# Modulation columns of a two-block transformer kernel: block transposes and row sums on VectorE, with one final TensorE sum for all 48 columns

## The chip, the cores and the metric

The kernel runs on one core of a Trainium2 chip. The metric is the device time of one execution in microseconds (us); lower is better. All data are float32 in memory. A core has a matrix engine (TensorE, "PE" in the profile, its weight loads "PEld"), a vector engine (VectorE, "DVE"), a scalar engine (ScalarE, "ACT"), a general engine (GpSimd, "POOL"), and a queue that issues most DMA transfers (SyncE, "SP"). Each engine works through its own list of instructions in order and waits at semaphores for the others.

## The reference, cut to what matters

Two transformer blocks follow one another on 512 tokens of width 1024. The second block begins by making six modulation vectors of width 1024 from a conditioning vector `c`:

```python
cond = jax.nn.silu(c)
for l in range(DEPTH):          # DEPTH = 1
    mod = cond @ ada_w[l] + ada_b[l]          # (1, 1024) @ (1024, 6144)
    shift_m, scale_m, gate_m, shift_f, scale_f, gate_f = jnp.split(mod[:, None, :], N_MOD, axis=-1)

    h = rms_norm_2(x, mix_norm_g[l]) * (1 + scale_m) + shift_m
    proj = h @ w_in[l] + b_in[l]
```

`ada_w` has 6144 columns: 48 groups of 128. `mod` depends on nothing of the first block, so the kernel computes it beside the first block's feed-forward part, and needs it when the second block's first normalisation starts.

## The kernel before

The activations are kept transposed, with channels on the 128 partitions and the 512 tokens along the free axis. The large products run in `tile` (lines 2135 to 2137): for each 128-row slice k, three matmuls with 512 columns, high weights with high activations, high weights with low activations, low weights with high activations. SP loads weights for two tiles at a time into `raw` (function `unit`), ScalarE makes the high part (`hi`, lines 855 and 1125) as soon as the tile four places back is done (`tile_done`), and GpSimd makes the low part (`lo`, line 788, counted by `lo_done`). There are two `raw` buffers and four pairs `w_hi`, `w_lo`.

The tiles that matter here are, in order: the output projection (tiles S_OUT, `into_split_norm(0)`), a normalisation done in halves, the up-projection of the first block (`ffn_pe`, two tiles per VectorE step in a loop of ten rounds with four tiles each), and the down-projection, 24 tiles numbered n = 0 to 23 (`down_part`, the last four in halves by `down_half`). Tile n = 18 has eight slices. Every sixth and fifth down tile is followed by `residual2` on VectorE (line 1822), ScalarE's `square2` (line 1155), and VectorE's `add_square2` (lines 1833, 1834). ScalarE does `square2` for n = 5, 6, 11, 12, 17 and 18 ahead of the `hi` of tile n + 4, in its fixed order.

The modulation works on column group n, from 0 to 47:

- SP loads 128 columns of `ada_w_2`, 1024 rows deep, into `ada[n % 2]`, 512 KB (`ada_load`, line 698). From n = 2 on it first waits until `ada_summed` has reached n - 1, that is until group n - 2 is reduced and its buffer free. These loads stand between the weight loads in SP's one list, so one that waits holds the next weight load back.
- VectorE (`ada_reduce`) multiplies the eight slices by their `cond` column and adds them: one TENSOR_SCALAR (line 1746), six SCALAR_TENSOR_TENSOR into PSUM bank 5 (line 1751), and one that writes the sum to SBUF as `ada_sum` (line 1756), after which `ada_summed` rises.
- TensorE (`ada_tile`, line 2440) sums over the partitions: `ada_sum` as weights against a column of ones. The result is one column of PSUM bank 6. The profile records it as two passes.

Groups 0 to 5 stand in the output projection and the normalisation, 6 to 27 in the up-projection (two per round), and 28 to 47 among the down tiles: VectorE reduces them at its steps n = 0 to 15, TensorE turns them into columns after tiles n = 0 to 17. Then VectorE waits for all 48 (`ada_done`), adds `ada_b_2` (line 1850) and makes the gains. Group 27 is the last one of the loop; `count` in the code is only the semaphore's value.

Of the kernel before, what the change touches and what calls it, by code (L numbers as in the profile page):

```python
# [10 lines left out]
ALU = mybir.AluOpType  # L11
ACT = mybir.ActivationFunctionType
AX = mybir.AxisListType


P = 128
# [142 lines left out]
def build(nc, a, out):  # L159
# [5 lines left out]
    with ctx:  # L165
# [100 lines left out]
        g_lo = sb("g_lo", [P, FT, T], F32R)  # L266
        ada_at = offset[0]
        ada = [sb(f"ada{n}", [P, KD, P], at=ada_at + 4096 * n) for n in range(2)]
        ada_sum = [sb(f"ada_sum{n}", [P, P], at=ada_at + 8192 + 512 * n) for n in range(2)]
        ua = sq  # L270
        uv = hn
        assert max(top1, ada_at + 9216) <= end
# [1077 lines left out]
        def _(dve):  # L1350
# [383 lines left out]
            def ada_reduce(n, loaded, i=None):  # L1734

                buf = n % 2
                count = lambda v: v if i is None else i * 2 + v

                acc = ps[5][:, 0:P]
                if n:  # L1740
                    dve.wait_ge(ada_summed, count(n))
                dve.wait_ge(ada_in[buf], loaded)
                for k in range(KD):
                    src, c = ada[buf][:, k, :], cond[:, k:k + 1]
                    if k == 0:
                        dve.tensor_scalar(acc, src, c, None, ALU.mult).then_inc(ada_scaled, 1)
                        continue
                    done = (KD - 1) * n + k
                    dve.wait_ge(ada_scaled, done if i is None else i * (2 * (KD - 1)) + done)
                    if k < KD - 1:  # L1750
                        dve.scalar_tensor_tensor(out=acc, in0=src, scalar=c, in1=acc, op0=ALU.mult,  # L1751
                                                 op1=ALU.add).then_inc(ada_scaled, 1)
                        continue
                    if n >= 2:
                        dve.wait_ge(ada_done, count(n - 1))
                    dve.scalar_tensor_tensor(out=ada_sum[buf][:, :], in0=src, scalar=c, in1=acc, op0=ALU.mult,
                                             op1=ALU.add).then_inc(ada_summed, 1)

            def ada_between_halves():
                dve.wait_ge(half_lo, KD)  # L1760
# [77 lines left out]
            for n in range(20):  # L1838
                if n % 6 >= 4:
                    dve.wait_ge(tile_done, S_DOWN + n + 1)  # L1840
                    residual2(n, slice(0, T)).then_inc(freed["dve"], 1)
                if n < 16:
                    for _ in range(2 if n % 4 == 2 else 1):
                        m = next(next_ada)
                        ada_reduce(m, 16 * (m // 2 + 1))
                if n >= 6 and n % 6 in (0, 1):
                    add_square2((n - 6) // 6 * 2 + n % 6)

            dve.wait_ge(ada_done, NMOD * KD)
# [282 lines left out]
        def _(pe):  # L2132
# [62 lines left out]
            def into_split_norm(b, x, xl, ready, after=lambda n: None):  # L2195

                s0 = SPLIT_FROM[b]
                if b == 2:

                    for part in ((0, 4), (4, KD)):  # L2200
                        for n in range(2):
                            tile(s0 + n, x, xl, part=part, ready=ready if n == 0 else None)
                for n in range(2 if b == 2 else 0, 4):
                    tile(s0 + n, x, xl, ready=ready if n == 0 else None)
                    after(n)
                for n in range(4, KD):
                    half_tile(b, s0 + n, 0, x, xl)
                    after(n)
# [11 lines left out]
            def parts(sem, base=0):  # L2220
                return lambda k: pe.wait_ge(sem, base + k + 1)
# [212 lines left out]
            for s in range(S_CONV, S_OUT):  # L2434
                tile(s, cv_hi, cv_lo, ready=parts(cv_lo_done) if s == S_CONV else None)

            def ada_tile(n, buf, count):

                pe.wait_ge(ada_summed, count)
                pe.matmul(ps[6][:, bass.ds(n, 1)] if not isinstance(n, int) else ps[6][:, n:n + 1],  # L2440
                          ada_sum[buf][:, :], ones[:, 0:1], start=True, stop=True).then_inc(ada_done, 1)

            def early_ada(tile_n):
                n = {1: 0, 2: 1, 3: 2, 5: 3, 6: 4}.get(tile_n)
                if n is not None:
                    ada_tile(n, n % 2, n + 1)

            into_split_norm(0, h_hi, h_lo, parts(freed["dve"], FREED[S_CONV][1] - 1), early_ada)

            def ffn_pe(s0, b):  # L2450
                for half in range(2):
                    for j in range(4):
                        if (half, j) == (1, 0):
                            second_halves(s0, h_hi, h_lo, lambda k: pe.wait_ge(half_lo, PIECES * b + KD + k + 1))
                        if half and j < 2:
                            continue
                        half_tile(b, s0 + j, half, h_hi, h_lo,
                                  ready=(lambda k: pe.wait_ge(half_lo, PIECES * b + KD * half + k + 1)) if j == 0 else None)
                        if (half, j) == (0, 1):
                            second_sum(b)  # L2460
                        if (half, j) == (1, 3) and b == 0:
                            ada_tile(ADA_EARLY - 1, (ADA_EARLY - 1) % 2, ADA_EARLY)
                with pe.Fori(0, FT // 2 - 1) as i:
                    for j in range(4):
                        s = s0 + 4 + j
                        pe.wait_ge(lo_done, i * 4 + (s + 1))
                        pe.wait_ge(freed["dve"], i * 4 + (FREED[s][1] - 4))
                        for k in range(KD):
                            ins = split_product(ps[BANK[s]][:, :], w_hi[s % 4][:, k, :], w_lo[s % 4][:, k, :],
                                                h_hi[:, k, :], h_lo[:, k, :], k == 0, k == KD - 1)  # L2470
                        ins.then_inc(tile_done, 1)
                        if b == 0 and j % 2:
                            n = ADA_EARLY + j // 2
                            ada_tile(i * 2 + n, n % 2, i * 2 + (n + 1))

            ffn_pe(S_UP, 0)

# [44 lines left out]
            next_ada = itertools.count(ADA_EARLY + ADA_UP - 2)  # L2522
            for n in range(20):
                down_part(S_DOWN, n, parts(g_lo_done, 2) if n in (0, 2, 4) else None)
                if n < 18:
                    for _ in range(2 if n and n % 4 == 0 else 1):
                        m = next(next_ada)
                        ada_tile(m, m % 2, m + 1)
            for n in range(20, 24):
                down_half(n, 0)  # L2530
            for n in range(20, 24):
# [248 lines left out]
```

## Time and profile before

| quantity | value |
|---|---|
| median of 3 runs | 1382.02 us (1380.93 to 1382.14) |
| profiled execution, its own time | 1381.31 us |
| span of the profiled execution | 1379.3 us |
| PE busy | 1367.5 us |
| DVE busy | 770.4 us |
| ACT busy | 599.2 us |
| POOL busy | 600.4 us |
| transfers over the span | 106 GB/s |

Busy time is a union over the span, so the engines overlap. Matmuls are pipelined, and their recorded durations overlap too; how long TensorE takes for a row of them is read from start to start.

### The profile page before, as it was taken

To read this page: it belongs to the slowest core of one execution; us is meant where nothing else is said; L and a number is where in the kernel's file an instruction comes from. 1 tells how busy PE (TensorE), PEld (TensorE's weight loads), DVE (VectorE), ACT (ScalarE), POOL (GpSimd) and SP (SyncE) were. 2 spreads that over 40 slices of the span, in tenths; PEclk is the share of its full clock that TensorE was granted. 3 is DMA by queue.
4 is the path that set the end of the run, shared out by engine and by line. 5 is a ranking of instruction groups with operands and counts; after the bars stand their busy time and mean duration, and the time that the engine had idled before them with its cause. 6 is when DMAs were issued, how large, how long until landed. Compare 5 with 4: busy or idle time off the path is not lost.

```text
span 1379.3 us, 20888 instructions
## 1 busy us (share of the span) xinstructions
PE 1367.5 (99%) x7650; PEld 1142.9 (83%) x7650; DVE 770.4 (56%) x1524; ACT 599.2 (43%) x1030; POOL 600.4 (44%) x322
## 2 busy tenths in 40 slices
PE   8999999999999999999999999999999999999998
PEld 7877777778998888888889978878998888888887
DVE  5897965456677566666873868633563223231222
ACT  6223555464254445443222524575364434442222
POOL 7532222226254444444543479623354444444441
PEclk9999999999999999999999999999999999999999
DMA  6931011015525444445662141021223332222221
GB/s 214 228 93 62 31 62 46 25 38 168 168 94 166 139 147 150 146 129 170 196 203 92 62 122 62 32 62 31 92 78 106 106 107 91 91 87 96 99 84 62
DMA packets 188309, 146.15 MB, mean 106 GB/s; under 512 B 21561, under 2 KB 186659, under 8 KB 188240
## 3 DMA queue, kind: packets, MB, share of 16 engines
q1 hardware_dynamic: 186528, 144.59, 34.0%
q8 instruction: 47, 0.77, 0.2%
q10 hardware_dynamic: 1200, 0.36, 0.1%
q0 software_dynamic: 512, 0.25, 0.1%
q14 instruction: 22, 0.18, 0.0%
HBM read 143.08 MB, written 2.10 MB: 105 GB/s over the span
## 4 chain that ended last, share of the span: by engine, by line
PE 91%; DVE 5%; DMA 3%; issue 1%; ACT 0%; DVEq 0%; ACTq 0%
PE ps L2135 27%; PE ps L2137 26%; PE ps L2136 26%; DMA ada<-in_ada_w 3%; DVE ps L1751 2%; PE ps L2584 2%; PE ps L2324 2%; PE ps L2379 1%; PE ps L2408 1%; PE ps L2655 1%; PE ps L2611 1%; PE ps L2640 1%; PE ps L2677 0%; PE ps L2218 0%; PE ps L2570 0%
## 5 line engine op out<-in xcount | busy, mean ns | idle before, releaser
L788 POOL TENSOR_TENSOR w_lo<-raw,w_hi 128x1024 fp32r<-128x1024 f32 (+2 forms) x224 | 515.4, 2304 | 709.0 <-ACT w_hi L855 439.4
L2135 PE MATMUL ps<-h_hi,w_hi 128*128 128x512 f32 (+1 forms) x1336 | 504.0, 377 | 0.6 <-DVE h_lo L1386 0.6
L2136 PE MATMUL ps<-h_lo,w_hi 128*128 128x512 f32 (+1 forms) x1336 | 493.4, 369 | 0.0
L2137 PE MATMUL ps<-h_hi,w_lo 128*128 128x512 f32 (+1 forms) x1336 | 493.2, 369 | 0.0
L2135 PEld LDWEIGHTS ps<-h_hi,w_hi 128*128 128x128 f32 x1336 | 251.7, 188 | 60.8 <-issue 17.6
L2137 PEld LDWEIGHTS ps<-h_hi,w_lo 128*128 128x128 f32 x1336 | 251.8, 188 | 43.1
L2136 PEld LDWEIGHTS ps<-h_lo,w_hi 128*128 128x128 f32 x1336 | 251.9, 189 | 40.1 <-issue 0.5
L855 ACT ACTIVATE w_hi<-raw 128x1024 fp32r<-128x1024 f32 (+2 forms) x136 | 133.7, 985 | 254.5 <-PE ps L2137 245.1
L1125 ACT ACTIVATE w_hi<-raw 128x1024 fp32r<-128x1024 f32 x88 | 93.2, 1059 | 217.9 <-PE ps L2137 217.9
L2135 PE MATMUL ps<-g_hi,w_hi 128*128 128x512 f32 (+1 forms) x394 | 146.6, 372 | 0.0
L2136 PE MATMUL ps<-g_lo,w_hi 128*128 128x512 f32 (+1 forms) x394 | 144.6, 367 | 0.0
L2137 PE MATMUL ps<-g_hi,w_lo 128*128 128x512 f32 (+1 forms) x394 | 144.4, 367 | 0.0
L1751 DVE SCALAR_TENSOR_TENSOR ps<-ada,cond,ps 128x128 f32<-128x128 f32 x288 | 102.5, 356 | 10.3
L2137 PEld LDWEIGHTS ps<-g_hi,w_lo 128*128 128x128 f32 x394 | 74.3, 188 | 12.2
L2135 PEld LDWEIGHTS ps<-g_hi,w_hi 128*128 128x128 f32 x394 | 74.3, 189 | 11.7
L2136 PEld LDWEIGHTS ps<-g_lo,w_hi 128*128 128x128 f32 x394 | 74.4, 189 | 11.5
L1790 DVE SCALAR_TENSOR_TENSOR sq<-ps,small,sq 128x511 f32<-128x511 f32 x44 | 33.0, 750 | 88.4 <-ACT sq L1132 85.4
L2060 DVE SCALAR_TENSOR_TENSOR xT<-ps,small,xT 128x256 f32<-128x256 f32 (+1 forms) x22 | 13.3, 604 | 106.1 <-PE ps L2137 106.1
L1527 DVE SCALAR_TENSOR_TENSOR ps<-z,small,ps 128x512 f32<-128x512 f32 x106 | 70.4, 747 | 0.0
L1784 DVE TENSOR_TENSOR hn<-ps,sq 128x512 f32<-128x512 f32 x22 | 15.2, 691 | 85.9 <-ACT sq L1136 85.9
L1022 ACT ACTIVATE sc<-sc,stat 128x128 f32<-128x128 f32 (+3 forms) x64 | 35.5, 555 | 35.0 <-DVE stat L1540 34.9
L1670 DVE COPY pT<-ps 128x128 f32<-128x128 f32 (+3 forms) x32 | 15.7, 490 | 54.3 <-PE ps L2379 32.1
(362 smaller groups left out, 1700.8 us busy)
## 6 DMA issues: line engine op xcount, KB each, us to landing
ada<-in_ada_w SPq DMA_DIRECT2D x48, 512.0 KB, 3.8
raw<-in_ffn_w_up SPq DMA_DIRECT2D x22, 1024.0 KB, 4.9
raw<-in_w_up SPq DMA_DIRECT2D x22, 1024.0 KB, 4.9
raw<-in_w_in SPq DMA_DIRECT2D x21, 1024.0 KB, 5.0
raw<-in_ffn_w_down SPq DMA_DIRECT2D x8, 896.0 KB, 6.2
raw<-in_w_down SPq DMA_DIRECT2D x8, 896.0 KB, 4.7
raw<-in_w_in SPq DMA_DIRECT2D x16, 256.0 KB, 3.8
raw<-in_w_out SPq DMA_DIRECT2D x4, 1024.0 KB, 5.2
```

Of the source, the lines that this page charges most:

```text
L788: pool.tensor_tensor(w_lo[slot % 4][:, 0:nk, :], part[:, :, slot % 2 * P:(slot % 2 + 1) * P], w_hi[slot % 4][:, 0:nk, :].bitcast(F32), ALU ...
L855: act.activation(w_hi[s % 4][:, 0:nk, :], part[:, :, s % 2 * P:(s % 2 + 1) * P], ACT.Copy).then_inc(hi_done, 1)
L1022: act.activation(x, x, ACT.Exp, scale=-1.0, bias=stat[:, 2 * (j % 2) + g:2 * (j % 2) + g + 1], accum_out=stat[:, 4 + 2 * (j % 2) + g:5 + 2 ...
L1125: act.activation(w_hi[s % 4][:, :, :], part[:, :, s % 2 * P:(s % 2 + 1) * P], ACT.Copy).then_inc(hi_done, 1)
L1527: ins = dve.scalar_tensor_tensor(out=out, in0=src, scalar=w, in1=was, op0=ALU.mult, op1=ALU.add)
L1751: dve.scalar_tensor_tensor(out=acc, in0=src, scalar=c, in1=acc, op0=ALU.mult, op1=ALU.add).then_inc(ada_scaled, 1)
L1790: dve.scalar_tensor_tensor(out=u[:, t, 1:T], in0=src[:, 0:T - 1], scalar=col(wname, m + wide), in1=u[:, t, 1:T], op0=ALU.mult, op1=ALU.add ...
L2135: pe.matmul(out_ap, w, x, start=first, stop=False, **kw)
L2136: pe.matmul(out_ap, w, xl, start=False, stop=False, **kw)
L2137: return pe.matmul(out_ap, wl, x, start=False, stop=last, **kw)
L2324: pe.matmul(ps[4 + g][:, 0:L], qT[grp, i, t * P:(t + 1) * P], kT[grp, b, 0:L], start=True, stop=True).then_inc(qk_done, 1)
L2584: ins = pe.matmul(bank[:, at:at + nq], keys[:, hd, t * P:(t + 1) * P], qd[n % 2][:, hd, q0:q0 + nq], start=True, stop=True)
```

## The change

`ada_reduce` keeps the whole sum in PSUM: the eighth slice is added there as well. VectorE then transposes the 128x128 sum in 32x32 blocks, into the second quarter of bank 5, and adds up the 32 elements of each row of a block, which leaves four numbers per partition. They go to PSUM bank 6, at column 256 + 4n, and `ada_summed` rises after that. The partition group j of 32 and the four columns together hold partial sums of the 128 outputs. After group 47, `ada_columns` copies the 192 numbers per partition to SBUF (`ada_parts`) and makes `stacked`, a 128x32 matrix of four identities of size 32, from `ident`. TensorE no longer runs `ada_tile`; after tile n = 18 `ada_sums` runs four matmuls with `stacked` as weights and 48 columns each, one for each 32 output partitions. SP's code is the same. The core of the diff:

```diff
-        ada_sum = [sb(f"ada_sum{n}", [P, P], at=ada_at + 8192 + 512 * n) for n in range(2)]
+        ada_parts = sb("ada_parts", [P, 4, NMOD * KD], at=ada_at + 8192)
+        stacked = sb("stacked", [P, 32], at=ada_at + 8192 + 4 * 4 * NMOD * KD)
...
-                acc = ps[5][:, 0:P]
+                acc, turned = ps[5][:, 0:P], ps[5][:, P:2 * P]
+                step = lambda k: (KD + 1) * n + k
+                wait_step = lambda k: dve.wait_ge(ada_scaled, step(k) if i is None else i * (2 * (KD + 1)) + step(k))
                 if n:
-                    dve.wait_ge(ada_summed, count(n))
+                    wait_step(0)
                 dve.wait_ge(ada_in[buf], loaded)
                 for k in range(KD):
...
-                    if k < KD - 1:
-                        dve.scalar_tensor_tensor(out=acc, in0=src, scalar=c, in1=acc, op0=ALU.mult,
-                                                 op1=ALU.add).then_inc(ada_scaled, 1)
-                        continue
-                    if n >= 2:
-                        dve.wait_ge(ada_done, count(n - 1))
-                    dve.scalar_tensor_tensor(out=ada_sum[buf][:, :], in0=src, scalar=c, in1=acc, op0=ALU.mult,
-                                             op1=ALU.add).then_inc(ada_summed, 1)
+                    wait_step(k)
+                    dve.scalar_tensor_tensor(out=acc, in0=src, scalar=c, in1=acc, op0=ALU.mult,
+                                             op1=ALU.add).then_inc(ada_scaled, 1)
+                wait_step(KD)
+                if n:
+                    dve.wait_ge(ada_summed, count(n))
+                dve.transpose(turned, acc).then_inc(ada_scaled, 1)
+                wait_step(KD + 1)
+                first = 2 * P + 4 * n
+                dve.tensor_reduce(ps[6][:, first:first + 4] if i is None else ps[6][:, bass.ds(i * 8 + first, 4)],
+                                  turned.rearrange("p (j c) -> p j c", c=32), AX.X, ALU.add).then_inc(ada_summed, 1)
+
+            def ada_columns():
+
+                dve.wait_ge(ada_summed, NMOD * KD)
+                dve.tensor_copy(ada_parts[:, :, :], ps[6][:, 2 * P:2 * P + 4 * NMOD * KD].rearrange("p (n j) -> p j n", j=4))
+                dve.tensor_reduce(stacked[:, :], ident[:, :].rearrange("p (i r) -> p r i", r=32), AX.X,
+                                  ALU.add).then_inc(ada_summed, 1)
...
+                if n == 16:
+                    ada_columns()
...
-            dve.wait_ge(ada_done, NMOD * KD)
+            dve.wait_ge(ada_done, 1)
...
-            def ada_tile(n, buf, count):
-
-                pe.wait_ge(ada_summed, count)
-                pe.matmul(ps[6][:, bass.ds(n, 1)] if not isinstance(n, int) else ps[6][:, n:n + 1],
-                          ada_sum[buf][:, :], ones[:, 0:1], start=True, stop=True).then_inc(ada_done, 1)
+            def ada_sums():
+
+                pe.wait_ge(ada_summed, NMOD * KD + 1)
+                for j in range(4):
+                    ins = pe.matmul(ps[6][32 * j:32 * (j + 1), 0:NMOD * KD], stacked[:, :], ada_parts[:, j, :],
+                                    start=True, stop=True)
+                ins.then_inc(ada_done, 1)
...
             for n in range(20):
                 down_part(S_DOWN, n, parts(g_lo_done, 2) if n in (0, 2, 4) else None)
-                if n < 18:
-                    for _ in range(2 if n and n % 4 == 0 else 1):
-                        m = next(next_ada)
-                        ada_tile(m, m % 2, m + 1)
+                if n == 18:
+                    ada_sums()
```

VectorE at the end of the down-projection, before: the last two groups (46 and 47), the residuals of tiles 16 and 17, and the squares.

```order
550 L1746 TENSOR_SCALAR ps<-ada_111,cond 128x128
551 L1751 SCALAR_TENSOR_TENSOR ps<-ada_111,cond,ps 128x128 x6
552 L1756 SCALAR_TENSOR_TENSOR ada_sum_113<-ada_111,cond,ps 128x128
553 L1746 TENSOR_SCALAR ps<-ada_112,cond 128x128
554 L1751 SCALAR_TENSOR_TENSOR ps<-ada_112,cond,ps 128x128 x6
555 L1756 SCALAR_TENSOR_TENSOR ada_sum_114<-ada_112,cond,ps 128x128
556 L1822 TENSOR_TENSOR xT<-ps,xT 128x512 x2
557 L1833 TENSOR_TENSOR rstd<-hn,rstd 128x512
```

The same place in the changed kernel, whose line numbers are a little higher.

```order
584 L1749 TENSOR_SCALAR ps<-ada_111,cond 128x128
585 L1752 SCALAR_TENSOR_TENSOR ps<-ada_111,cond,ps 128x128 x7
586 L1757 STREAM_TRANSPOSE ps<-ps 128x128
587 L1760 TENSOR_REDUCE ps<-ps 128x4
588 L1749 TENSOR_SCALAR ps<-ada_112,cond 128x128
589 L1752 SCALAR_TENSOR_TENSOR ps<-ada_112,cond,ps 128x128 x7
590 L1757 STREAM_TRANSPOSE ps<-ps 128x128
591 L1760 TENSOR_REDUCE ps<-ps 128x4
592 L1833 TENSOR_TENSOR xT<-ps,xT 128x512
593 L1766 COPY ada_parts<-ps 128x192
594 L1767 TENSOR_REDUCE stacked<-ident 128x32
595 L1833 TENSOR_TENSOR xT<-ps,xT 128x512
```

Each group has two VectorE instructions more, and the copy and the reduction of `ada_columns` stand between the residuals of tiles 16 and 17.

TensorE after down tile n = 16, before: the columns of groups 45 and 46 stand between the last matmul of tile 16 and the first of tile 17.

```order
2239 L2137 MATMUL ps<-g_hi,w_lo_57 128x512
2240 L2440 MATMUL ps<-ones,ada_sum_114 128x1
2241 L2440 MATMUL ps<-ones,ada_sum_113 128x1
2242 L2135 MATMUL ps<-g_hi,w_hi_54 128x512
2243 L2136 MATMUL ps<-g_lo,w_hi_54 128x512
```

TensorE in the changed kernel, between tile n = 18 and tile n = 19, the only place where it does something for the modulation.

```order
2252 L2149 MATMUL ps<-g_lo,w_hi_51 128x512
2253 L2150 MATMUL ps<-g_hi,w_lo_55 128x512
2254 L2452 MATMUL ps<-ada_parts,stacked 32x48 x4
2255 L2148 MATMUL ps<-g_hi,w_hi_52 128x512
2256 L2149 MATMUL ps<-g_lo,w_hi_52 128x512
```

The 48 small products that were spread over the first block's second half are gone, and four others wait in one place for all 48 groups.

## Rows read from the trace of the kernel before

**Rows 1.** The page: busy us (share of the span) x instructions of each engine.

```profile
PE 1367.5 (99%) x7650; PEld 1142.9 (83%) x7650; DVE 770.4 (56%) x1524; ACT 599.2 (43%) x1030; POOL 600.4 (44%) x322
```

**Rows 2.** Timeline of PE around one column: start us, duration us, instruction, count.

```profile
432.56 0.39 PE L2137 MATMUL ps<-h_hi,w_lo 128*128 128x512 f32 x1
432.79 0.28 PE L2440 MATMUL ps<-ones,ada_sum 128*128 128x1 f32 x2
432.93 0.48 PE L2135 MATMUL ps<-h_hi,w_hi 128*128 128x512 f32 x1
...
433.48 0.39 PE L2137 MATMUL ps<-h_hi,w_lo 128*128 128x512 f32 x1
...
439.61 0.39 PE L2137 MATMUL ps<-h_hi,w_lo 128*128 128x512 f32 x1
```

**Rows 3.** Waits of PE and PEld, 340 to 740: us in total, times, longest.

```profile
PEld ps L2440 <- DVE ada_sum L1756: 1.3, 2, 1.0
```

**Rows 4.** The chain that ended last, 700 to 737: start us, us, what.

```profile
724.14 0.36 DVE ada_sum L1756
724.54 0.38 PE ps L2440 x2
```

**Rows 5.** Timeline of DVE in the down-projection; in brackets idle us and releaser.

```profile
642.72 0.35 DVE L1746 TENSOR_SCALAR ps<-ada,cond 128x128 f32<-128x128 f32 x1
643.10 2.32 DVE L1751 SCALAR_TENSOR_TENSOR ps<-ada,cond,ps 128x128 f32<-128x128 f32 x6
645.46 0.35 DVE L1756 SCALAR_TENSOR_TENSOR ada_sum<-ada,cond,ps 128x128 f32<-128x128 f32 x1
...
649.04 0.35 DVE L1756 SCALAR_TENSOR_TENSOR ada_sum<-ada,cond,ps 128x128 f32<-128x128 f32 x1
649.48 0.35 DVE L1746 TENSOR_SCALAR ps<-ada,cond 128x128 f32<-128x128 f32 x1
...
654.93 0.35 DVE L1746 TENSOR_SCALAR ps<-ada,cond 128x128 f32<-128x128 f32 x1 [2.36 <-DMA ada<-in_ada_w]
...
675.40 0.35 DVE L1746 TENSOR_SCALAR ps<-ada,cond 128x128 f32<-128x128 f32 x1 [2.98 <-DMA ada<-in_ada_w]
...
699.35 0.35 DVE L1746 TENSOR_SCALAR ps<-ada,cond 128x128 f32<-128x128 f32 x1 [3.29 <-DMA ada<-in_ada_w]
...
708.37 0.35 DVE L1746 TENSOR_SCALAR ps<-ada,cond 128x128 f32<-128x128 f32 x1 [2.34 <-DMA ada<-in_ada_w]
...
727.98 0.35 DVE L1756 SCALAR_TENSOR_TENSOR ada_sum<-ada,cond,ps 128x128 f32<-128x128 f32 x1
728.24 0.69 DVE L1822 TENSOR_TENSOR xT<-ps,xT 128x512 f32<-128x512 f32 x1
```

**Rows 6.** Waits of DVE, 636 to 735: us in total, times, longest.

```profile
DVE ps L1746 <- DMA ada<-in_ada_w: 13.0, 8, 3.3
```

**Rows 7.** Waits of DVE in the up-projection's loop, 405 to 636.

```profile
DVE hn L1790 <- ACT hn L1132: 47.3, 20, 3.8
```

**Rows 8.** Groups of DVE by line: busy us, mean ns, idle us before.

```profile
L1602 DVE TENSOR_REDUCE stat<-cp 128x8 f32<-128x248 f32 x4 | 1.6, 411 | 0.1
L1569 DVE COPY hn<-ps 127x128 f32<-127x128 f32 x2 | 0.5, 278 | 0.0
```

**Rows 9.** Timeline of PE: the first matmul of down tile 19.

```profile
735.38 0.39 PE L2135 MATMUL ps<-g_hi,w_hi 128*128 128x512 f32 x1
```

**Rows 10.** The chain that ended last, 3 to 12: start us, us, what.

```profile
3.56 4.99 PE ps L2218 x22
...
9.83 0.45 PE ps L2218 x4
```

**Rows 11.** Windows: us, busy by engine (x), PEclk, DMA share, GB/s.

```profile
4.00:5.00 1.00, 1.00 (x7) 1.00 (x6) 0.00 (x0) 0.50 (x1) 1.00 (x3) 1.00 1.01 406
```

**Rows 12.** Timeline of ACT where a square waits for VectorE's residual.

```profile
703.07 0.63 ACT L1155 ACTIVATE hn<-xT 128x512 f32<-128x512 f32 x1 [5.46 <-DVE xT L1822]
```

**Rows 13.** Timeline of POOL: the low weights made after that square.

```profile
704.70 2.11 POOL L788 TENSOR_TENSOR w_lo<-raw,w_hi 128x896 fp32r<-128x896 f32 x1 [3.88 <-ACT w_hi L855]
```

More of the change, by code:

```diff
@@ L1747, in ada_reduce @@
                         continue
-                    done = (KD - 1) * n + k
-                    dve.wait_ge(ada_scaled, done if i is None else i * (2 * (KD - 1)) + done)
-                    if k < KD - 1:
-                        dve.scalar_tensor_tensor(out=acc, in0=src, scalar=c, in1=acc, op0=ALU.mult,
-                                                 op1=ALU.add).then_inc(ada_scaled, 1)
-                        continue
-                    if n >= 2:
-                        dve.wait_ge(ada_done, count(n - 1))
-                    dve.scalar_tensor_tensor(out=ada_sum[buf][:, :], in0=src, scalar=c, in1=acc, op0=ALU.mult,
-                                             op1=ALU.add).then_inc(ada_summed, 1)
+                    wait_step(k)
[14 more added lines that the diff above has]
+                                  ALU.add).then_inc(ada_summed, 1)
             def ada_between_halves():
@@ L2193, in second_sum, with into_split_norm @@
                 pe.matmul(ps[7][:, COLS[1]], ones[:, :], rstd[:, COLS[1]], start=True, stop=True).then_inc(summed, 1)
-            def into_split_norm(b, x, xl, ready, after=lambda n: None):
+            def into_split_norm(b, x, xl, ready):
                 s0 = SPLIT_FROM[b]
@@ L2204, in into_split_norm @@
                     tile(s0 + n, x, xl, ready=ready if n == 0 else None)
-                    after(n)
                 for n in range(4, KD):
                     half_tile(b, s0 + n, 0, x, xl)
-                    after(n)
                 for n in range(4, KD):
@@ L2435, in _ @@
                 tile(s, cv_hi, cv_lo, ready=parts(cv_lo_done) if s == S_CONV else None)
-            def ada_tile(n, buf, count):
-                pe.wait_ge(ada_summed, count)
-                pe.matmul(ps[6][:, bass.ds(n, 1)] if not isinstance(n, int) else ps[6][:, n:n + 1],
-                          ada_sum[buf][:, :], ones[:, 0:1], start=True, stop=True).then_inc(ada_done, 1)
[L2443 to L2448, printed above, removed]
+            def ada_sums():
[4 more added lines that the diff above has]
+                ins.then_inc(ada_done, 1)
+            into_split_norm(0, h_hi, h_lo, parts(freed["dve"], FREED[S_CONV][1] - 1))
             def ffn_pe(s0, b):
@@ L2460, in ffn_pe @@
                             second_sum(b)
-                        if (half, j) == (1, 3) and b == 0:
-                            ada_tile(ADA_EARLY - 1, (ADA_EARLY - 1) % 2, ADA_EARLY)
                 with pe.Fori(0, FT // 2 - 1) as i:
@@ L2471, in ffn_pe @@
                         ins.then_inc(tile_done, 1)
-                        if b == 0 and j % 2:
-                            n = ADA_EARLY + j // 2
-                            ada_tile(i * 2 + n, n % 2, i * 2 + (n + 1))
             ffn_pe(S_UP, 0)
@@ L2520, in turn_inverse @@
                 ins.then_inc(inverses_turned, 1)
-            next_ada = itertools.count(ADA_EARLY + ADA_UP - 2)
             for n in range(20):
                 down_part(S_DOWN, n, parts(g_lo_done, 2) if n in (0, 2, 4) else None)
-                if n < 18:
-                    for _ in range(2 if n and n % 4 == 0 else 1):
-                        m = next(next_ada)
-                        ada_tile(m, m % 2, m + 1)
+                if n == 18:
+                    ada_sums()
             for n in range(20, 24):
```

## The prediction

> **What bounds the kernel now.** I read the page first: TensorE is busy for 1367.5 of 1379.3 us, VectorE for 770.4 [rows 1], so work taken from TensorE comes off the time unless someone else takes over as the last. Next the timeline of TensorE around one modulation column, for what a column costs there: the reader is to look at the starts, since durations overlap [rows 2]. Then the waits, for where TensorE already stood still for the modulation: two weight loads waited for VectorE's sum, 1.3 us in all, and nothing larger waits there between 340 and 740 [rows 3]. Small as that is, the chain that ended last shows what it means: it runs through VectorE's last operation of a group at 724.14 into TensorE's column at 724.54 [rows 4]. So in the down-projection VectorE's row of reductions and TensorE end nearly together: VectorE had no lead there. The last view is VectorE's own timeline and waits in that stretch [rows 5, 6]. Some of its reductions wait for their load: 13.0 us in eight waits [rows 6], of which four long ones are 2.36, 2.98, 3.29 and 2.34 [rows 5], 10.97 us together, so that the other four are 2.0 us together.
>
> **What TensorE is relieved of.** Ordinary matmuls follow one another at (439.61 - 433.48) / 27 = 0.227 us. From the matmul before a column (432.56) to the third one after it (433.48) are 0.92 us instead of 3 x 0.227 = 0.68 [rows 2]. A column costs 0.24 us, and 48 cost 11.5 us. The two waits add 1.3 [rows 3]. Left alone, TensorE would start down tile 19 at 735.38 [rows 9] - 12.8 = 722.6.
>
> **What VectorE takes on.** Before, a group runs from the start of its first operation at 642.72 to the end of the last, 645.46 + 0.35 = 645.81: 3.09 us. Inside, a dependent operation of this size starts (645.46 - 643.10) / 6 = 0.39 us after the one before it, with 0.35 of its own: 0.04 us between an end and the next start [rows 5]. The eighth operation stays, now into PSUM. The transposition and the row sum are new, and the trace of before shows neither at this size. The nearest rows are a copy of 128 columns out of PSUM, 0.278 us, and a TENSOR_REDUCE of 248 columns, 0.411 us [rows 8]. The row sum of 128 columns lies between 0.411 x 128/248 = 0.21 and 0.411; I take 0.28, as the copy of 128 columns, whose data are of this size. For the transposition I take 0.30 between the copy's 0.278 and the 0.35 of an operation with a column of scalars [rows 5, 8]; that it runs at half the copy's rate, so up to about twice 0.278, is not excluded. With two gaps of 0.04 the sum is 0.30 + 0.28 + 0.08 = 0.66; since ends in PSUM may come later I take **0.70 us a group**, bounds 0.5 (two times 0.21 and the gaps) and 1.05 (0.56 + 0.41 + 0.08).
>
> The Trainium skill (VectorE: DVE Perf Modes, "The three transpose paths") gives 311 ns for a 128x128 bf16 transposition in blocks, by which a group would cost 0.67. Its "Rules for kernel authors" advise TensorE for 128x128 and warn that `tensor_reduce` is the slowest operation of the engine; no run here has shown that yet.
>
> **Where that is hidden, and where not.** In the up-projection's loop VectorE waits 47.3 us in 20 waits, 3.8 at most, for ScalarE and so for TensorE's tiles [rows 7]; that is over 2 us a wait against 0.70 that comes in front of it. The cost of groups 0 to 27 is covered there and in the normalisation; without this cover each would cost 0.70. TensorE's gain is real until then: VectorE enters the down-projection with the tile that TensorE finished at 633, 25 columns earlier, so 25 x 0.24 = 6.0 us earlier.
>
> In the down-projection 21 groups (27 to 47) follow almost without pause. Only SP's loads loosen the row. SP issues the load of group k when group k - 2 is reduced, so a reduction that was gated by its load inherits the delay of k - 2 and not of k - 1. That gives back one 0.70 at each of the four long waits, 2.8, and at the four short ones only the wait itself, 2.0. Where one group directly follows another, the new group's first operation need no longer wait for the end of the sum (0.44 us from 649.04 to 649.48 [rows 5]), only for the transposition; against the 0.26 between 727.98 and 728.24 [rows 5] that saves 0.18 a time, at four places 0.7. The delay that VectorE gathers is
>
> 21 x 0.70 - 2.8 - 2.0 - 0.7 = 9.2 us,
>
> and 9.2 - 6.0 = 3.2 us later than before its last group is done: 727.98 + 0.35 + 3.2 = 731.5. Behind it come the residual of tile 16 (0.69 [rows 5], of which 0.6 before the next can start), the copy of 192 columns and the reduction for `stacked`, 0.3 each by the same rows: **732.7**. Only then may TensorE run `ada_sums`. It came to that place at 722.6, so it stands still for about 10 us: the gain of 12.8 is turned into a wait. What is queued behind it is tile 19, the last four tiles in halves and everything after.
>
> ScalarE's squares also wait for VectorE's residuals, ahead of the next `hi` in its list. Before, such a square started at 703.07 after 5.46 us of waiting [rows 12], and the low weights behind it were ready at 704.70 + 2.11 = 706.8 [rows 13], 3.7 later. With VectorE's delay of about 7 at that point, less 6, the square comes near 704 to 705 and the weights near 708 to 709; they are for tile 16, which TensorE, free of its columns, reaches at 707 to 708. That is a microsecond or two of waiting before the large wait, which becomes as much shorter: it costs nothing more. SP's weight loads wait behind modulation loads that come later by the same delay; the buffers hold weights for two pairs of tiles ahead, and VectorE's delay against TensorE is smaller than a pair of tiles takes (48 x 0.227 = 10.9 us), so I count nothing. VectorE's reading of `mod` has slack until the halves of tile 22.
>
> **After the wait.** The four products cost 4 x 0.24 = 1.0 us by the columns of before. Tile 19 would start at 733.8 instead of 735.38: 1.6 us gained. But TensorE after 10 us of rest is unlike TensorE at work: at the start of the program, after 3.3 us without work, 22 matmul passes took 4.99 us, 0.227 each, and four of the same kind later took 0.45 us, 0.112 each [rows 10]. The granted clock in the window row reads 1.00 there [rows 11], so here the spacing shows the lower rate and the clock column does not. Half rate for 5 us costs 2.5 us. Nothing in the second half of this trace shows a rest of 10 us, so the bounds are 0 and 2.5; I take the 2.5, by the nearest row. The sum is -1.6 + 2.5 = **+0.9 us** against the profiled execution's own 1381.31 us (span 1379.3), and against the median, which is 0.7 above that execution, 1382.9.
>
> The Trainium skill (TensorE: Matmul & The Clock Gate, "HAM oscillation — how this bites in real kernels") says that idle gaps of the matrix engine put its clock back to the lower of its two levels, 1.2 instead of 2.4 GHz; by that rule the 2.5 us is due, and without it the kernel gains 1.6. The start of this trace agrees in the spacing.
>
> **Rivals.**
> - *The cost of a group is higher.* Each 0.1 us above 0.70 a group adds 21 x 0.1, less 0.4 at the four long waits and some 0.3 at the short ones, which then give back more: 1.4 us. At 0.85 the sum is +3.0, at 1.05 it is +5.8: 1385 to 1388. For it: neither operation is in the trace. Against it: the copy and the reduction that are there are cheap. It decides from 0.84 us a group.
> - *The clock does not fall*, or only shortly: -1.6, or 1380.4; with a group at 0.55 also -3.7, or 1378.3. For it: the granted clock reads 1.00 everywhere. Against it: rows 10.
> - *Faster: the sums stay off the path.* If VectorE's delay were covered, because loads come sooner once SP is relieved or because a group costs hardly more than before, TensorE would keep its 12.8 less 1.0 for `ada_sums`: -11.8, or 1370.2. It needs VectorE to be ready at 722.6, with its last group 6 us before where it now stands and before the copy, while all 8 waits for loads are only 13.0 us. Against it stands that VectorE was already the later one [rows 3, 4].
> - *The wait breaks something behind it*: weights for tiles 20 to 23 late through ScalarE's squares, some 2 to 4 us more. For it: the squares of tiles 16 and 17 stand in ScalarE's list before the weights of tiles 21 and 22. Against it: tile 21 follows the wait by more than tile 19's 24 x 0.227 = 5.4 us, and those weights need 3.7.
>
> **How the numbers follow.** 0.2% of this time is 2.8 us, about what a measurement can tell from no change. The forecast case (a group at 0.6 to 0.83, lower rate after the wait) runs from -0.5 to +2.8: chance 0.42, nearly all "same". Dearer groups 0.28 and the broken wait 0.05: slower. No fall of the clock 0.15, half of it within 0.2%. Off the path 0.10. Same 0.47, slower 0.33, faster 0.20. The range goes from groups at 0.5 with the clock kept (-1.6 - 2.8, or 1377.6) to groups at 1.05 with TensorE's half rate (1388); the forecast case alone is 1381.5 to 1384.8.
>
> **What the profile after would show.** TensorE's instructions 96 passes fewer and 8 more, and its loop round 0.48 us shorter: right if VectorE's entry into the down-projection is 6 us earlier. The transposition near 0.30 and the row sum near 0.28. VectorE's waits for loads down from 13.0 us to some 8 or 9. One long wait of PE for VectorE's `stacked`, 8 to 11 us, ending near 733, and behind it matmuls at twice the 0.227 for up to 5 us. The prediction is wrong if the wait is under 5 us or over 15, if a group costs under 0.5 or over 1.05, or if the matmuls behind the wait run at 0.227 from the first.

## The result

The changed kernel took 1373.97 us (median of 6 runs, 1372.26 to 1376.49) against 1380.73 us for the kernel before in the same series; the ratio is 0.9945, 95% interval 0.9935 to 0.9956. A second series gave 1375.10 against 1381.81, ratio 0.9943 (0.9931 to 0.9956). The change makes the kernel 0.55% faster, some 7 us. The forecast was 1382.9, no change that can be told.

The page of the profiled execution (its own time 1372.39 us), which answers to [rows 1]:

```profile
span 1370.7 us, 20826 instructions
PE 1357.2 (99%) x7562; PEld 1132.7 (83%) x7562; DVE 802.8 (59%) x1622; ACT 598.4 (44%) x1030; POOL 601.6 (44%) x322
```

TensorE has 88 passes fewer (96 less 8), and 10.3 us less of busy time. VectorE has 98 instructions and 32.4 us more.

VectorE's timeline in the down-projection, as in [rows 5]: groups 29 and 30, then two places where the kernel before waited for a load, then the end of group 47 and what follows it.

```profile
640.81 0.35 DVE L1749 TENSOR_SCALAR ps<-ada,cond 128x128 f32<-128x128 f32 x1
641.20 2.71 DVE L1752 SCALAR_TENSOR_TENSOR ps<-ada,cond,ps 128x128 f32<-128x128 f32 x7
643.94 0.33 DVE L1757 STREAM_TRANSPOSE ps<-ps 128x128 f32<-128x128 f32 x1
644.30 0.30 DVE L1760 TENSOR_REDUCE ps<-ps 128x4 f32<-128x128 f32 x1
644.51 0.35 DVE L1749 TENSOR_SCALAR ps<-ada,cond 128x128 f32<-128x128 f32 x1
...
693.28 0.35 DVE L1749 TENSOR_SCALAR ps<-ada,cond 128x128 f32<-128x128 f32 x1
...
701.27 0.35 DVE L1749 TENSOR_SCALAR ps<-ada,cond 128x128 f32<-128x128 f32 x1
...
723.25 0.30 DVE L1760 TENSOR_REDUCE ps<-ps 128x4 f32<-128x128 f32 x1
723.46 0.68 DVE L1833 TENSOR_TENSOR xT<-ps,xT 128x512 f32<-128x512 f32 x1
724.06 0.35 DVE L1766 COPY ada_parts<-ps 128x192 f32<-128x192 f32 x1
724.32 0.37 DVE L1767 TENSOR_REDUCE stacked<-ident 128x32 f32<-128x128 f32 x1
```

A group now lasts from 640.81 to 644.60, 3.79 us instead of 3.09: the 0.70 of the forecast, with 0.33 for the transposition and 0.30 for the row sum. But group 47 ends at 723.55, where the forecast had 731.5. The two rows at 693.28 and 701.27 are groups 41 and 43: there the kernel before waited 3.29 and 2.34 us for the load [rows 5], and here no bracket stands behind them.

VectorE's waits for loads between 636 and 735, in the form of [rows 6] (us in total, times, longest):

```profile
DVE ps L1749 <- DMA ada<-in_ada_w: 3.2, 4, 1.5
```

TensorE's wait for VectorE's last sum, from its waits between 636 and 745, in the form of [rows 3]:

```profile
PE ps L2452 <- DVE stacked L1767: 3.0, 1, 3.0
```

TensorE's timeline at the final products, between tiles 18 and 19:

```profile
721.34 0.39 PE L2150 MATMUL ps<-g_hi,w_lo 128*128 128x512 f32 x1
724.75 0.29 PE L2452 MATMUL ps<-ada_parts,stacked 128*32 128x48 f32 x8 [3.02 <-DVE stacked L1767]
724.97 0.50 PE L2148 MATMUL ps<-g_hi,w_hi 128*128 128x512 f32 x1
725.31 0.40 PE L2149 MATMUL ps<-g_lo,w_hi 128*128 128x512 f32 x1
```

Tile 19 starts at 724.97 instead of 735.38 [rows 9], 10.4 us earlier. Of these 0.7 were there before the change could act: this execution started its first products that much sooner. So the change had won 9.7 us here. The eight passes cost 0.22 us from start to start and not 1.0; they have 32 columns of weights each where the passes of before had 128, but no run here tries that width by itself.

1.6 us went again later. The chain that ended last, near 943:

```profile
942.67 0.43 PE ps L2149
943.10 0.43 PE ps L2150
```

And the window row from 942 to 945, in the form of [rows 11] (in the last column but two the granted clock, the share of TensorE's full rate that it was given):

```profile
942.00:945.00 3.00, 3.00 (x8) 2.35 (x8) 0.28 (x1) 1.91 (x4) 0.00 (x0) 0.50 0.00 0
```

The matmuls follow at 0.43 us instead of 0.23, and the granted clock is 0.50 of full speed, the 1.2 GHz level; before came 24 recorded passes with one column each.

### The profile page after: what moved, and what is told of

Its sections match the earlier page's. It is cut to its first block, busy times and chain, and to the rows that moved or that the text cites. A ratio compares the mean times of both kernels' runs of the same rounds, so it can differ in the third digit from the quotient of the medians.

```text
span 1370.7 us, 20826 instructions
## 1 busy us (share of the span) xinstructions
PE 1357.2 (99%) x7562; PEld 1132.7 (83%) x7562; DVE 802.8 (59%) x1622; ACT 598.4 (44%) x1030; POOL 601.6 (44%) x322
## 4 chain that ended last, share of the span: by engine, by line
PE 90%; DVE 7%; DMA 2%; issue 1%; ACT 0%; DVEq 0%; SPq 0%; ACTq 0%
PE ps L2148 26%; PE ps L2149 26%; PE ps L2150 26%; DVE ps L1752 3%; PE ps L2584 2%; PE ps L2335 2%; PE ps L2390 1%; DMA ada<-in_ada_w 1%; PE ps L2419 1%; PE ps L2655 1%; PE ps L2611 1%; PE ps L2640 1%; DMA x_in<-in_x 0%; PE ps L2677 0%; DVE ps L1757 0%
## 5 line engine op out<-in xcount | busy, mean ns | idle before, releaser
L1752 DVE SCALAR_TENSOR_TENSOR ps<-ada,cond,ps 128x128 f32<-128x128 f32 x336 | 119.6, 356 | 12.0
L2073 DVE SCALAR_TENSOR_TENSOR xT<-ps,small,xT 128x256 f32<-128x256 f32 (+1 forms) x22 | 13.3, 604 | 106.2 <-PE ps L2150 106.2
```

## The experiments

In each, the "row" is VectorE's stretch from the start of group 27 to the end of group 47, read from its timeline, and "load waits" are the waits inside it. "Residuals and squares" are VectorE's eleven operations with 512 columns between these groups: four residuals and seven steps of squares. Theory A: VectorE's extra work is swallowed by the load waits, because loads also land sooner. Theory B is the rule on record, that a load wait gives back one group's extra cost at most. Theory C is chance from one execution to the next.

| kernel | row us | load waits us | residuals and squares us | median flight us | PE waits for a sum us | ratio to before (95%) |
|---|---|---|---|---|---|---|
| before | 88.8 | 13.0 | 11.9 | 4.5 | 1.3 | 1 |
| before_again | 88.5 | 13.5 | 11.2 | 4.3 | 1.0 |  |
| changed | 90.8 | 3.2 | 9.5 | 3.9 | 3.0 | 0.9945 (0.9935 to 0.9956) |
| after_again | 90.6 | 2.3 | 10.0 | 4.1 | 2.9 | 0.9943 (0.9931 to 0.9956) |
| pe_only | 80.7 | 8.8 | 8.1 | 4.1 | 0 | 0.9913 (0.9896 to 0.9929) |
| dve_only | 90.1 | 3.6 | 8.6 | 3.9 | 2.5 | 1.0036 (1.0023 to 1.0048) |
| swapped | 84.3 | 4.7 | 8.7 | 3.8 | 0 | 0.9988 (0.9978 to 0.9997) |
| slow | 98.5 | 0.5 | 13.1 | 4.1 | 10.8 | 0.9988 (0.9978 to 0.9999) |
| sums19 | 90.8 | 1.9 | 11.1 | 4.0 | 0 | 0.9903 (0.9886 to 0.9919) |
| sums19_again | 95.1 | 3.7 | 13.3 | 4.1 | 1.9 | 0.9913 (0.9897 to 0.9929) |
| early_release | 85.7 | 0.8 | 7.5 | 3.9 | 0 | 0.9921 (0.9895 to 0.9947) |
| both | 85.7 | 0.6 | 7.5 | 4.0 | 0 | 0.9908 (0.9891 to 0.9924) |

The flight is a modulation load's time from issue to landing, the median of those issued between 640 and 722. In the kernels that keep TensorE's columns, its waits are those of its weight loads. The five columns before the ratio are of one profiled execution each.

The steps of squares are not of one length, and the traces show with what they change: with GpSimd's making of low weights (`w_lo`). From the kernel before, a residual, with one of its two inputs in PSUM, and a step of a square, with both in SBUF, each beside such an operation; and the same step in the changed kernel:

```profile
660.83 2.12 POOL L788 TENSOR_TENSOR w_lo<-raw,w_hi 128x896 fp32r<-128x896 f32 x1 [1.14 <-ACT w_hi L855]
661.05 0.68 DVE L1822 TENSOR_TENSOR xT<-ps,xT 128x512 f32<-128x512 f32 x1
682.58 2.39 POOL L788 TENSOR_TENSOR w_lo<-raw,w_hi 128x1024 fp32r<-128x1024 f32 x1 [1.89 <-ACT w_hi L855]
682.80 2.73 DVE L1833 TENSOR_TENSOR rstd<-hn,rstd 128x512 f32<-128x512 f32 x1
...
678.08 2.40 POOL L789 TENSOR_TENSOR w_lo<-raw,w_hi 128x1024 fp32r<-128x1024 f32 x1 [2.29 <-ACT w_hi L856]
679.68 1.35 DVE L1844 TENSOR_TENSOR rstd<-hn,rstd 128x512 f32<-128x512 f32 x1
```

Over the 12 profiles, between 636 and 735, 49 steps of squares start while a `w_lo` operation runs: each ends 0.28 to 0.55 us after that operation, and they last up to 2.9 us. The other 80 last 0.48 to 0.75 us. The residuals last 0.68 to 0.69 us, also the twelve that start while a `w_lo` operation runs. So the squares' part of the row depends on how long they meet GpSimd's low weights.

**before_again: the kernel before once more.**

> The unchanged kernel once more. If the load waits of the row are a matter of chance from one execution to the next, they differ from 13.0 us by several us here, and the duration of the row from 88.8 us. If they belong to the program, both stay within 1 us, and so do the landing times of the single loads (6.9 us for group 41, 5.8 for group 43).

The group of modulation loads in the DMA issues from 640 to 722 in the first profile of the kernel before, with the median flight last:

```profile
ada<-in_ada_w SPq DMA_DIRECT2D x19, 512.0 KB, 4.5
```

The same group in before_again:

```profile
ada<-in_ada_w SPq DMA_DIRECT2D x19, 512.0 KB, 4.3
```

And in the changed kernel:

```profile
ada<-in_ada_w SPq DMA_DIRECT2D x18, 512.0 KB, 3.9
```

Row and load waits come out within 0.5 us of the first profile, and so do the flights of groups 41 and 43 (6.4 and 5.9 us instead of 6.9 and 5.8). They belong to the program, and theory C falls for the kernel before, as far as two profiles can tell. What did differ was the clock: this execution dropped to half rate at 952.7 for eleven matmuls and lost 3.2 us against the first one, where the first one did not.

**dve_only: only VectorE's part of the change.** From the kernel before, with TensorE's columns kept; the edit cut to its core, arguments and semaphore steps left out:

```diff
-                    dve.scalar_tensor_tensor(out=ada_sum[buf][:, :], ...).then_inc(ada_summed, 1)
+                    dve.scalar_tensor_tensor(out=ada_sum[buf][:, :], ...).then_inc(ada_scaled, 1)
+                dve.transpose(turned, ada_sum[buf][:, :]).then_inc(ada_scaled, 1)
+                dve.tensor_reduce(ps[5][:, first:first + 4], ...).then_inc(ada_summed, 1)
```

> The kernel before, TensorE's 48 columns kept, but VectorE transposes and row-sums each group as in the change (the four numbers go unused to another bank). By the rule on record (a load wait gives back only one group's extra cost) the row of 21 reductions grows by about 9 us, and TensorE, which waits for each group, is held: 8 to 9 us slower. By the rival (the extra work is swallowed by the 13.0 us of load waits, because loads land sooner when they are spaced wider) the row grows by about 2 us, load waits fall from 13.0 to about 3, and the kernel is 1 to 3 us slower.

VectorE's waits for loads between 636 and 735 in this kernel (us in total, times, longest):

```profile
DVE ps L1748 <- DMA ada<-in_ada_w: 3.6, 5, 1.6
```

VectorE's load waits fell to the 3.6 us of this line, and 21 x 0.70 = 14.7 us more work lengthened the row by 1.3 us. Theory B had 9. The load waits gave back 9.4 us of it; the residuals and squares, shorter by 3.3 us, gave back most of the rest, which theory A did not have. In the profiled execution TensorE reached tile 19 by 1.2 us later than before, counted from its first products; the median over executions is 4.7 us later (1385.31 against 1380.61), which is what neither theory gave (1 to 3, and 8 to 9). The profile shows a drop of the clock near 953 for 1.6 us of the rest. For the remaining 2 us of the median there is no profile; the mean granted clock of these executions was 0.996 to 0.998, that of the kernel before 0.998 to 1.000, so part of it may be lower clock elsewhere.

**pe_only: only TensorE's part.** 47 of the 48 columns are left out, so the second block gets wrong modulation; VectorE works as before, without its waits for the columns. The part of the edit in the down-projection; the columns of groups 0 to 27 are taken out in the same way:

```diff
-                if n < 18:
-                    for _ in range(2 if n and n % 4 == 0 else 1):
-                        m = next(next_ada)
-                        ada_tile(m, m % 2, m + 1)
+                if n == 18:
+                    ada_tile(NMOD * KD - 1, (NMOD * KD - 1) % 2, NMOD * KD)
```

> The kernel before, with VectorE's work as it was, but TensorE makes no modulation column except the last one, after down tile 18 (47 of 48 columns are left out, so the second block is computed with wrong modulation). Both theories agree here: TensorE loses 47 x 0.24 = 11.3 us and its 1.3 us of waits; VectorE's row of 21 reductions in the down-projection, from the start of group 27 to the end of group 47, stays at its 88.8 us within 1.5 us and begins 6 us earlier, so TensorE does not wait at the last column. About 12.5 us faster than before, less what the lower clock takes elsewhere (0 to 3 us).

1368.74 us against 1380.61, 11.9 us faster; in the profile TensorE stood 12.95 us earlier from tile 19 to the end, by the sum 47 x 0.24 + 1.3 = 12.6. The price of the columns was right. The row was not: its work is that of before, and it shrank from 88.8 to 80.7 us. Load waits fell by 4.2 us, and the residuals and squares took 8.1 instead of 11.9 us. What differs for the row is when TensorE's tiles, and with them SP's weight loads and GpSimd's low parts, come beside it.

**swapped: order and spacing of the loads alone.** The kernel before, SP's order in the down-projection changed:

```diff
-                if m % 2:
-                    unit((S_DOWN + 7 + m) // 2)
                 for _ in range(2 if m % 4 == 2 else 1):
                     k = next(next_ada)
                     if k < NMOD * KD:
                         ada_load(k)
+                if m % 2:
+                    unit((S_DOWN + 7 + m) // 2)
```

> The kernel before with one change in SP's list for the down-projection: the weight load of every second step stands behind that step's modulation load instead of ahead of it. VectorE's and TensorE's work is the same. If the loads of before land late because the next modulation load leaves 1 to 3 us behind a weight load (which is my theory of what wider spacing cured in the changed kernel), the mean flight of the loads of the row falls from 4.7 us to about 4.2, load waits from 13.0 to 8 or less, the row from 88.8 us by 3 us or more, and TensorE's 1.3 us of waits vanish: 1 us faster, not more. If spacing is not the cause, flights and waits stay within 1 us.

The waits of VectorE between 636 and 735 in this kernel that bear on the row:

```profile
DVE xT L1822 <- PE ps L2137: 7.0, 3, 4.1
DVE ps L1746 <- DMA ada<-in_ada_w: 4.7, 7, 0.8
DVE ada_sum L1756 <- PE ps L2440: 4.2, 4, 1.5
```

No operation of any compute engine was added or taken away, and the load waits fell from 13.0 to 4.7 us, the row to 84.3, although 7.1 us of it are now waits for TensorE (4.2 for its columns, 2.8 for its tiles), which the row did not have before; the squares took 3.2 us less. TensorE's 1.3 us of waits are gone; the kernel gained 0.12%, as expected. So the load waits depend on when the loads leave. SP's timeline shows it, in the kernel before around group 41, whose load had a flight of 6.9 us:

```profile
689.21 0.37 SPq L698 DMA_DIRECT2D ada<-in_ada_w  x1
690.20 0.37 SPq L688 DMA_DIRECT2D raw<-in_ffn_w_down  x1
692.40 0.37 SPq L698 DMA_DIRECT2D ada<-in_ada_w  x1
```

and in the changed kernel, where group 41's load had a flight of 3.9 us:

```profile
685.42 0.37 SPq L699 DMA_DIRECT2D ada<-in_ada_w  x1
685.83 0.58 SPq L689 DMA_DIRECT2D raw<-in_ffn_w_down  x1
689.11 0.37 SPq L699 DMA_DIRECT2D ada<-in_ada_w  x1
```

Before, a modulation load followed the 896 KB weight load by 2.2 us. In the changed kernel the weight load leaves 0.4 us behind the modulation load that held it back, and the next one comes 3.3 us later. Over the row, those that come next behind a weight load do so after 1.1 to 4.1 us before (one after 6.1), and after 3.3 to 4.7 us now; their flights average 5.3 us before and 4.4 now, those of the others 4.3 and 4.0. Not every flight follows this: group 43's took 5.8 us before with the last weight load 12.3 us ahead of it, and why is not shown.

**slow: more work than the waits can take.** The changed kernel with one more transposition in groups 28 to 47.

```diff
+                if i is None and n >= 28:
+                    link(dve.transpose(ps[5][:, 2 * P:3 * P], acc))
                 dve.transpose(turned, acc).then_inc(ada_scaled, 1)
```

> The changed kernel with one more 32x32-block transposition (into spare columns) in each of groups 28 to 47: 20 x 0.37 = 7.4 us more for VectorE in a row that has only 3.2 us of load waits left. The rival theory: the row grows from 90.8 by 5 to 7 us, TensorE's wait for the final sum grows from 3.0 to 8 to 10 us, and the kernel is 5 to 7 us slower than the changed one. The rule on record gives the same within 1 us. On the clock: if a rest of 8 to 10 us lowers it, the matmuls behind the wait follow at 0.43 us and the granted clock reads 0.5, for a further 1.5 to 2.5 us; after the 3.0 us rest of the changed kernel they followed at 0.23.

Two windows of this kernel around the final products; the columns are the stretch, the busy time of PE, PEld, DVE, ACT and POOL with their counts, the granted clock, the DMA share and GB/s:

```profile
722.00:732.00 10.00, 0.00 (x0) 0.00 (x0) 9.19 (x28) 0.05 (x1) 0.00 (x0) 0.63 0.45 144
732.00:737.00 5.00, 4.48 (x18) 3.51 (x19) 4.90 (x6) 2.78 (x4) 3.50 (x2) 0.50 0.05 10
```

These windows show TensorE at rest for 10 us (its wait is 10.8) and then at a granted clock of 0.50, the 1.2 GHz level; the matmuls followed at 0.43 us until 738.1. The matmuls of tile 19 and those behind it lost some 2.5 us to it, against the changed kernel's first profile. The row grew by 7.7 us for 7.4 us of work, and that is partly luck: the load waits gave back 2.7 us of the work, and the squares took 3.6 us more, since more of them ran beside GpSimd's low weights. 1379.46 us is 5.5 above the changed kernel's 1373.97. This kernel is what the forecast had described.

**after_again: the changed kernel once more.**

> The changed kernel once more, beside the version with the final products after tile 19 on the same chip. Ratio to before 0.9935 to 0.9956 as first measured; TensorE's wait for the final sum again 3.0 us within 0.5, the row 90.8 us within 1, load waits 2 to 3.5 us. The drop of the granted clock near 943 us may be there or not: it was there in one of two profiles of the kernel before.

Three windows of this execution, with the same columns:

```profile
720.00:725.00 5.00, 3.26 (x15) 2.37 (x13) 4.52 (x14) 0.00 (x0) 0.00 (x0) 1.00 0.62 214
725.00:727.00 2.00, 0.86 (x9) 0.70 (x10) 2.00 (x5) 1.43 (x3) 0.00 (x0) 0.64 0.00 0
727.00:730.00 3.00, 3.00 (x8) 2.32 (x7) 2.90 (x3) 1.41 (x3) 2.88 (x2) 0.50 0.00 0
```

Row and waits agree with the first profile. But here the clock did fall behind the wait of 2.9 us, to 0.50, and twelve matmuls at 0.43 us, with the slower start before them, cost about 2.7 us. After 3.0 us of wait in the first profile it had not. The rest near 725 is thus a risk of some 2.7 us in some executions, beside the one near 945. This profile also has a lower clock from 15.5 to 19.0 us, at the program's start, and its products were 1.6 us later than in the first profile from there on.

**sums19: the final products one tile later.**

```diff
-                if n == 18:
+                if n == 19:
                     ada_sums()
```

> The changed kernel with the four final products one tile later, after down tile 19. TensorE comes there 5.4 us later than before, at about 727.2, when VectorE's part has been ready since 724.7: the 3.0 us wait disappears and nothing takes its place, since VectorE still has 3.8 us of waiting for TensorE behind the gains. By both theories 3.0 us faster than the changed kernel, so about 1370.5 to 1371.

1369.09 us, no wait for the sum in the profile. TensorE stood 12.7 us ahead of the kernel before from there (13.3 less 0.5 at the start), 3.2 more than the changed kernel at the same place in its first profile.

> The final products after tile 19, on the same chip as the changed kernel: 3.0 us, or 0.22%, under it.

1369.94 against 1375.10 us for the changed kernel on the same chip, 5.2 us (4 us by the ratios to the kernel before) where the wait alone gives 3.0. The intervals are too wide to call the excess certain. What fits it is the lower clock behind the wait: after_again's profile lost 2.7 us to it, and the mean granted clock was 0.995 to 0.998 in the 11 executions of the changed kernel and 0.997 to 1.000 in the 10 with the later place. It is not shown for the executions without a profile. The row was 95.1 us in this profile, 4.3 longer than in the other one of the same kernel, with load waits of 3.7 instead of 1.9 us and 2.2 us more in the residuals and squares, and TensorE waited 1.9 us, with the granted clock at 1.00 behind it. For the changed kernels the row's length does differ from one execution to the next; to that extent theory C holds.

**early_release: loads leave before the transposition and the row sum.** The load in the up-projection's loop is changed in the same way.

```diff
-                    sp.wait_ge(ada_summed, n - 1 if count is None else count)
+                    sp.wait_ge(ada_scaled, (KD + 1) * (n - 2) + KD if count is None else count)
```

> The changed kernel, but SP's loads wait for the eighth slice (ada_scaled) and no longer for the row sum: each load leaves 0.7 us earlier. The theory: VectorE's row loses most of its 3.2 us of load waits, ends 2 to 3 us earlier and TensorE's wait for the final sum falls from 3.0 to 0 to 1 us: 2 to 3 us faster than the changed kernel. The rival: earlier loads meet the weight loads again, flights grow from 4.1 us towards 4.7, and the wait stays above 2 us.

The row fell by 5.1 to 85.7 us, load waits to 0.8, flights stayed at 3.9, and TensorE did not wait. 2.4 us of the 5.1 are load waits and 2.0 are residuals and squares (7.5 instead of 9.5 us), which I had not expected. 1370.29 us, with executions from 1367.66 to 1375.21.

**both: early release and the later place.**

> Early release and the final products after tile 19 together. If the wait of TensorE is all that VectorE's row costs, early release adds nothing to the later place: the same time as with the later place alone, within 0.5 us, that is 3.0 us faster than the changed kernel. If VectorE's lateness also costs elsewhere (weights held behind modulation loads), both together are faster still.

1369.33 us, as the later place alone: within what these series can tell, TensorE's wait was all that the row cost. Of the versions tried, sums19 and both are the fastest, 0.9 to 1.0% under the kernel before and 0.3 to 0.4% under the changed one. Early release shortened the row by 5 us in its profile and in that of both; sums19_again, whose row was 4.3 us longer, shows that such a reserve can be of use.

## Why the prediction was wrong

The step that failed is the one in "Where that is hidden, and where not": "The delay that VectorE gathers is 21 x 0.70 - 2.8 - 2.0 - 0.7 = 9.2 us". Measured are 90.75 - 88.81 = 1.9 us. The flights of the loads were kept as the trace had them, and a change in the squares was put at nothing. Point by point:

- *What TensorE is relieved of*: right. 12.8 us on record, 12.6 by pe_only's sum, 12.95 measured.
- *The cost of a group*: right, 0.70 on record; 0.71 on the mean of the 21 groups, 15.0 us in all. The 0.7 us for groups that follow one another directly was right too: 0.8.
- *The up-projection hides it*: right. VectorE entered the down-projection 6.7 us earlier, 0.7 of that from the start of the execution, and TensorE gained 0.24 us with each column up to there.
- *What the load waits give back*: wrong. On record 2.8 + 2.0 = 4.8 us, measured 13.0 - 3.2 = 9.8 us. I had kept every load's flight as it was and let a gated group inherit the delay of the group two before. Flights belong to the order and spacing of the issues: with VectorE slower, a weight load leaves together with a modulation load, and the next one leaves 3.3 us or more behind it, where before it could be 1.1. dve_only shows it with TensorE's work kept, swapped with the work of all engines kept. The rule on record can be replayed group by group with the issue at the end of group k - 2. With the flights and squares of the kernel before and the longer groups it gives a row longer by 9.7 us, near the 9.2 on record; with the changed kernel's flights 4.3, and with its squares too 1.9. These are estimates from the rows of the two profiles, and they put some 5.4 us of the error on the flights and 2.4 on the squares.
- *What I left out*: the residuals and squares took 11.9 us before, 9.5 in the changed kernel, 8.1 in pe_only, by how many met GpSimd's low weights. That is 2.4 us more, which the forecast had not looked for. The sum closes: 15.0 - 9.8 - 2.4 - 0.8 = 2.0, against 1.9.
- *The wait at the final products*: 3.0 us instead of 10, by the same error. `ada_sums` cost 0.2 instead of 1.0.
- *The half rate after the rest*: right for a rest of 10.8 us (2.5 us measured, 2.5 on record), and a matter of the execution for a rest of 3 us: none in one profile, 2.7 us in the other. The Trainium skill (TensorE: Matmul & The Clock Gate, "HAM oscillation") describes this chain, a wait that lets the clock drop so that the next products start slow; the rests of 10.8 and 2.9 us agree with it, the one of 3.0 us does not, nor that of 1.9 us in sums19_again.

So at tile 19 the sum is -12.8 + 3.0 + 0.2 = -9.6 us, against -9.7 in the profile; 1.6 us at 943 take it to 8.1. The median gained 7; the fall behind the wait in other executions, as after_again shows one, would account for the rest, but has no profile in this series. The faster rival, that loads come sooner and cover VectorE's delay, was right in its reason and too far in its size: it had no wait at all and 11.8 us of gain, 1370.2.

## What to carry to other kernels

When extra work goes to an engine whose row is loosened by waits for transfers, do not keep the flights of the trace: list what each transfer follows in its queue, before and after, since a slower consumer also spaces the issues. Then work out the growth of the row for both ends, all waits kept and all waits gone (here 14.7 and 14.7 - 13.0 = 1.7 us). That the measured 1.9 lies beside the second is partly luck: the waits gave back 9.8 and not 13.0, and shorter squares and closer groups the rest; dve_only, at 1.3, lies under it. So look also at what the operations of the row share with another engine, for their length moves with it. A wait that remains should be looked at for where it stands: moved by one tile it vanished in one of two profiles and was 1.9 us in the other, without a lower clock behind it.

## What was not expected of the hardware

- The granted clock falls to 0.50 behind 24 passes with one column each, in 7 of 12 profiles of these kernels (between 939 and 954) and not in the other 5; the kernel before is among both kinds. In two profiles (after_again and swapped) it also fell from 15.5 to 19.0 us. The fall behind the 24 passes cost 1.6 us in six of the profiles and 3.2 in before_again, about as much as executions of one kernel lie apart. In the two profiles of the changed kernel TensorE has no recorded wait between 900 and 950.
- A rest of TensorE of 3.0 us left the clock as it was in one execution, a rest of 2.9 us lowered it in another of the same kernel.
- 128x512 operations of VectorE that read SBUF alone took from 0.5 to 2.9 us: those that started while GpSimd made low weights ended 0.28 to 0.55 us after it, all 49 of them, while the residuals, with one input in PSUM, kept their 0.68 us beside it. The second kind of square averaged 1.49 us over five in one profile of sums19 and 2.23 us over four in the other.
